# The mixture-of-experts stage of a two-block network on one core: expert by expert over all tokens, or token-expert pairs sorted into blocks of 128 slots

## The reference, cut to what matters

```python
grp_logits = t @ w_grp + b_grp                      # 4 groups
g_sel      = top_k(grp_logits, 1)
p_grp      = softmax(grp_logits)[g_sel]
in_grp     = (t @ w_exp + b_exp)[g_sel]             # 8 experts of the group chosen
top_val, top_idx = top_k(in_grp, 2)
top_w      = softmax(top_val) * p_grp
...
for gi in range(4):                                 # 8 experts each, 32 in all
    hid = silu(t @ w1[gi]) * (t @ w3[gi])           # 1024 -> 256 per expert
    out = out + (hid * gate[:, gi]) @ w2[gi]        # 256 -> 1024
h = h + g2 * out;  return rmsnorm_2(h, final_norm)
```

## Time and profile before

| | us |
|---|---|
| median of 3 runs | 3089.29 |
| lowest, highest | 3083.87, 3097.57 |
| span of the profiled execution | 3076.1 |
| median less span: launch and end, outside the records | 13.2 |
| stage of the experts, router to the end of the last `down` | 2503.8 to 3059.1 |
| tail, from there to the end of the span | 3059.1 to 3076.1 |

### The profile page before, as it was taken

One profiled execution on the slowest core, in us unless ns is written; L12 is line 12 of the kernel. 1 busy time (PEld: TensorE's weight loads), 2 busy tenths in 40 slices (PEclk: granted clock), 3 DMA queues, 4 the chain that ended last, 5 costly groups with the idle time before them and its releaser, 6 DMA issues.

```text
span 3076.1 us, 59430 instructions
## 1 busy us (share of the span) xinstructions
PE 2952.3 (96%) x19108; PEld 2680.6 (87%) x19108; DVE 2087.5 (68%) x3812; ACT 1582.8 (51%) x3113; POOL 1342.8 (44%) x1069
## 2 busy tenths in 40 slices
PE   7999999988999998999999799999999999999998
PEld 6689999986778877999999777878899889999997
DVE  7647963358888877589203888888654557777777
ACT  1125554468555555555555865555564335555554
POOL 5733888887544420069898855444000010000100
PEclk8999999999999998999999999999999999999999
DMA  6634556731666642445567037665354345555554
GB/s 247 214 105 152 183 195 249 271 131 55 253 232 230 227 139 70 139 151 184 180 209 259 27 141 267 234 226 203 131 183 136 120 137 192 191 193 192 202 191 144
DMA packets 153464, 552.60 MB, mean 180 GB/s; under 512 B 16896, under 2 KB 19712, under 8 KB 153232
## 3 DMA queue, kind: packets, MB, share of 16 engines
q1 hardware_dynamic: 151136, 547.42, 51.8%
q10 hardware_dynamic: 2224, 3.87, 0.4%
HBM read 550.17 MB, written 1.05 MB: 179 GB/s over the span
## 4 chain that ended last, share of the span: by engine, by line
PE 80%; ACT 8%; DVE 4%; POOL 3%; issue 3%; DMA 1%; ACTq 0%; DVEq 0%; POOLq 0%; SPq 0%
PE bank L1042 22%; PE bank L1012 21%; PE bank L1295 12%; PE bank L746 9%; PE bank L1316 5%; PE bank L805 5%; ACT hT L1528 3%; POOL w_parts L2656 2%; ACT hT L1524 1%; PE bank L770 1%; ACT h_parts L1536 1%; PE bank L691 1%; POOL arena L2704 1%; DMA ring<-stream 1%; PE bank L833 1%
## 5 line engine op out<-in xcount | busy, mean ns | idle before, releaser
L2656 POOL TENSOR_TENSOR w_parts<-ring,w_parts 128x512 fp32r<-128x512 f32 x512 | 660.6, 1308 | 407.6 <-ACT w_parts L1488 376.1
L1012 PE MATMUL bank<-h_parts,w_parts 128*128 128x256 f32 x6144 | 751.8, 284 | 6.0 <-ACT arena L1424 4.4
L1012 PEld LDWEIGHTS bank<-h_parts,w_parts 128*128 128x128 f32 x6144 | 743.3, 193 | 7.0 <-issue 4.8
L1488 ACT ACTIVATE w_parts<-ring 128x512 fp32r<-128x512 f32 x512 | 319.6, 631 | 344.5 <-PE bank L1012 273.7
L1710 ACT ACTIVATE w_parts<-ring 128x512 fp32r<-128x512 f32 x384 | 242.0, 632 | 262.6 <-PE bank L1295 129.9
L1295 PEld LDWEIGHTS bank<-h_parts,w_parts 128*128 128x128 f32 x3072 | 373.4, 192 | 2.6 <-issue 0.2
L1295 PE MATMUL bank<-h_parts,w_parts 128*128 128x256 f32 x3072 | 374.4, 283 | 0.0
L2586 DVE TENSOR_TENSOR w_parts<-ring,w_parts 128x512 fp32r<-128x512 f32 x376 | 273.1, 739 | 145.3 <-ACT w_parts L1710 142.0
L1042 PE MATMUL bank<-w_parts,a_parts 128*128 128x512 f32 x1536 | 370.6, 397 | 0.4 <-DVE a_parts L2291 0.4
L1042 PE MATMUL bank<-h_parts,a_parts 128*128 128x512 f32 x1536 | 365.3, 393 | 5.0 <-DVE a_parts L2291 5.0
L1042 PEld LDWEIGHTS bank<-h_parts,a_parts 128*128 128x128 f32 x1536 | 284.7, 188 | 78.2 <-DVE a_parts L2291 20.4
(11 more groups left out here) (347 smaller groups left out, 4455.5 us busy)
## 6 DMA issues: line engine op xcount, KB each, us to landing
ring<-stream SPq DMA_DIRECT2D x786, 512.0 KB, 3.4
arena<-stream SPq DMA_DIRECT2D x144, 512.0 KB, 4.3
hT<-stream SPq DMA_DIRECT2D x80, 512.0 KB, 4.6
mean<-stream SPq DMA_DIRECT2D x32, 512.0 KB, 4.5
arena<-consts ACTq DMA_DIRECT2D x1, 1536.0 KB, 6.4
xT<-xin ACTq DMA_DIRECT2D x1, 1024.0 KB, 10.7
out<-hT SPq DMA_DIRECT2D x4, 256.0 KB, 2.2
arena<-subk ACTq DMA_DIRECT2D x2, 128.0 KB, 2.1
```

The costliest lines, as they stand in the source:

```text
L1012: mm = pe.matmul(bank[k][:, 0:T], w[:, wp, ws], h_parts[:, hp, 4 * j + q, :], start=(j == 0 and q == 0 and i == 0), stop=(j == 1 and q == ...
L1488: act.activation(w_parts[half % HALVES][:, 0, :], ring[slot_][:, j * 512:(j + 1) * 512], ACT.Copy).then_inc(sem(f"{n}_high"), 1)
L2656: pool.tensor_tensor(w[:, 1, :], ring[(base + k) % RING][:, j * 512:(j + 1) * 512], w[:, 0, :].bitcast(F32), ALU.subtract).then_inc(sem(f" ...
```

## The change

The 512 pairs are given slots 0 to 511 in the order of their experts, and the slots are cut into four blocks of 128. An expert's pairs can lie on both sides of a boundary between blocks. There are three boundaries, so there are 32 + 3 = 35 steps, each of one expert and one block. Which expert and block a step has is computed on the chip; the number of steps is fixed.

- **Before the steps.** The tokens are transposed (16 transposes) and split. Five small products with a matrix of ones and a strictly triangular one (`below`) count the pairs ahead of each pair. VectorE makes one-hot matrices `E.first` and `E.sort` from these positions (256 tokens x 512 slots), and a table of integers `E.steps`. TensorE gathers the tokens into slot order with 32 fp32r matmuls of 512 columns; the result goes to `E.xs`, high part by ScalarE, low part by VectorE. There are 24 and 8 calls of `keep_clock` between.
- **A step.** Now the block's 128 slots stand in the array and the weights move through: 24 fp32r matmuls of 512 columns give all of x·w1 and x·w3. VectorE multiplies silu, the gate of the slot and the other half in one operation. Two transposes turn the hidden values, and w2 is multiplied in plain float32, 4 products of 512 columns. VectorE adds the result into the block's part of `E.y`. GpSimd copies the next block's tokens (`E.xb`, two copies of 128 x 1024).
- **Loads.** w1 and w3 of a step come in one transfer of 2 MB, w2 in one of 1 MB. Each has two buffers. Their rows in `stream` are read from `E.steps` into a register (`value_load`) by SP. VectorE and GpSimd read their block from it likewise.
- **After the steps.** `E.y` is split and multiplied with the transposed `E.sort`, 8 matmuls of 256 columns for each of 8 chunks, in the place of the two transposes a chunk.

The loops over steps below are SP's, TensorE's, ScalarE's, VectorE's and GpSimd's, in this order.

```diff
+BLOCKS = TT * 2
+STEPS = NE + BLOCKS - 1
+PARTED = 3
...
+            def up_load(p, row):
+
+                sp.dma_start(E.raw[:, p % 2].rearrange("p h s n -> p s (h n)"), stream[row].rearrange("s p n -> p s n"))\
+                  .then_inc(sem(f"v_landed{p % 2}"), 16)
...
+            for p in range(3, STEPS):
+                row = step_row(UP_ROW, p)
+                sp.wait_ge(sem("e_low"), 2 * p - 4)
+                up_load(p, bass.ds(row, 4))
+                row = step_row(DOWN_ROW, p - 1)
+                sp.wait_ge(sem("e_down"), 2 * (p - 2))
+                down_load(p - 1, bass.ds(row, 2))
+                if p in MOE_ROWS_AT:
+                    mod_load(MODS_MOE, MODS_MOE[0] + MOE_ROWS_AT[p])
...
+            keep_clock(pe, 24)
+            pe.matmul(t[:, 0:NE], ones, E.both[:, 0, :], start=True, stop=False)
...
+            keep_clock(pe, 8)
...
+                for q in range(4):
...
+                    for i, (x, wp) in enumerate(((0, 0), (0, 1), (1, 0))):
+                        mm = pe.matmul(o, step_x(p, x, 4 * h + q), E.hl[u % PARTED][:, wp, :, q * P:(q + 1) * P],
+                                       start=(h == 0 and q == 0 and i == 0), stop=(h == 1 and q == 3 and i == 2))
...
+            for p in range(STEPS):
+                if p + 1 < STEPS:
+                    up(p + 1, 0)
+                turned(p)
+                if p + 1 < STEPS:
+                    up(p + 1, 1)
...
+                down(p)
...
+            for p in range(STEPS):
+                silu(p)
+                if 2 * p + 4 < UNITS:
+                    high(2 * p + 4)
+                hidden_turned(p)
+                if 2 * p + 5 < UNITS:
+                    high(2 * p + 5)
...
+            for p in range(STEPS):
+                hidden(p)
+                if 2 * p + 4 < UNITS:
+                    low(2 * p + 4)
+                if p:
+                    add_up(p - 1)
+                if 2 * p + 5 < UNITS:
+                    low(2 * p + 5)
...
+            for p in range(1, STEPS):
+                at = pool.value_load(E.steps[0:1, SLOT_AT, p:p + 1], min_val=0, max_val=(BLOCKS - 1) * P)
+                if p >= 2:
+                    pool.wait_ge(sem("e_half"), 2 * (p - 1))
+                for x in range(2):
+                    ins = pool.tensor_copy(E.xb[:, p % 2, x, :, :], E.xs[x][:, :, bass.ds(at, P)])
```

More of the change, by code:

```diff
@@ L116 @@
            ("decay", RH * 384)]
+CONSTS_E = [("slots", 512), ("below", 128)]
 def offsets(table):
@@ L1341, in _ @@
+            for c in (DC - 2, DC - 1):
+                square_sum_pe(pe, "out", c)
         @block.tensor
@@ L1734, in moe_act @@
             act.wait_ge(sem("e_gexp"), signalled("e_gexp"))
-            highs(range(2, 3), same, same)
+            high(0)
             act.wait_ge(sem("e_vx"), 1)
```

562 lines of the change are left out of this document (346 added, 216 removed).

## The result

The kernel after takes 2908.40 us (median of 4 runs, 2906.18 to 2910.65) against 3086.58 for the kernel before in the same runs (3082.32 to 3097.57). The ratio is 0.9422, with a 95% interval of 0.9393 to 0.945: 5.8% faster. The forecast was 2934, with a range of 2903 to 3015. As a difference it was 155.7 us less; the medians differ by 178.2 and the two profiled spans by 169.2.

A forecast was written before the change was run, and what follows sets the result against it. TensorE was taken to bound the changed stage, with VectorE then setting 10.0 us a step. Lead-in, first step, 34 steps and tail made the span 155.7 us less; 3089.3 - 155.7 gave about 2934 us, range 2903 to 3015.

The forecast's parts named there:

- first step and gates: Start of the steps: two units of 2.82, 16 plain products (6.2) and 8 transposes (1.4), 13.2 us.
- 34 steps, last turn and `down`: Expert steps: 34 x 10.0 us, and 4.3 for the last turn and `down` with their wait.
- tail: After the last `down`: last addition and splits 2.1, eight chunks 11.5, 8.3 after the last square sum; 21.9 us.
- time less span: Whole kernel: the median lies 13.2 us above the profiled span, added at the end.
- VectorE's sum: Step on VectorE: 6.8 us, plus 2.0 for subtractions stretched by GpSimd's copies and 1.2 for register reads, 10.0 us.
- TensorE alone, 9.44: Rival for the steps: TensorE sets 9.44 us a step, 19 us less, 2915; chance 0.50 together with the forecast.
- TensorE's own step: Step on TensorE: 24 wide products 5.63, `down` 3.45, two transposes 0.36; 9.44 us against 16.98 an expert.
- The transfers: Steps, DMA: 8.7 to 9.5 us a step, close behind the limit; as rival setting the step 2971 us, chance 0.17.
- VectorE locked out: Rival for the steps: every GpSimd copy excludes every subtraction, 11.9 us a step, 65 more, 2999 us; chance 0.24.
- The slower rival: 2 MB loads: pieces 512 KB apart run below the ring's rate; 3288 us if nothing overlapped, chance 0.06.
- The lead-in: Between router and steps: first `up` at 2541.0 against 2512.2, 28.8 us lost.
- the signs named: Steps' profile: 9.9 to 10.1 us, TensorE near 95%, DMA share above 0.85; wrong if landings exceed 12 us.

The follow-up runs named there:

- experiment 1: Against the change: GpSimd's copies of the next block's tokens left out, with TensorE's wait for them; 2911.1 us, step 9.316 us.
- experiment 7: Against the change: VectorE's two register reads a step left out, gate and block taken by step number; 2912.6 us, step 9.416 us.
- experiment 4: Against the change: half of the `down` products and all matrix loads after the third step left out; 2853.7 us, step 7.886 us.
- experiment 2: Against the change: matrices loaded only for the first steps, modulation rows kept; 2904.9 us, step 9.180 us.
- Experiments 2 and 5: The second of these, against the change: two further plain products of 256 columns a step on TensorE, results unread; 2936.0 us, step 10.007 us.
- experiment 8: Against the change: the w2 load issued by ScalarE's queue instead of SP's; 2906.7 us, step 9.233 us.
- 10 to 12: The last of these, 12, is the kernel of experiment 11 run again, unchanged; 2900.1 us, step 9.249 us.
- experiment 6: Against the change: the 2 MB load as four transfers of 512 KB, each contiguous; 2915.9 us, step 9.367 us.
- experiment 3: Against the change: half of the `down` products left out, all loads kept; 2890.6 us, step 8.905 us.
- experiment 9: Against the change: before the steps, GpSimd's four subtractions wait until positions are known, 11 clock-keeping products instead of 24; 2911.8 us.
- experiment 11: Against the change: first two units split during the mixer, memset after the gates, 11 clock-keeping products, w2 load by ScalarE's queue; 2892.6 us.
- experiment 10: Against the change: the edits of experiment 8 and experiment 9 together; 2905.0 us, step 9.180 us.

## Why the prediction was right, point by point

The forecast was right: 2908.4 lies in the range, near its low end and 25.6 under the forecast. The reason held that TensorE had bound the stage and has 128 slots instead of 256 tokens to compute; that VectorE would take over as the limit did not. Term by term, in us:

| term | predicted | measured |
|---|---|---|
| router's start | 2503.80 | 2507.95 |
| from there to the first `up` | 37.2 | 39.1 |
| first step and gates | 13.2 | 10.0 |
| 34 steps, last turn and `down` | 344.3 | 325.3 |
| tail | 21.9 | 24.5 |
| time less span | 13.2 | 1.8 |

The rows add up: 4.15 + 1.9 - 3.2 - 19.0 + 2.6 = -13.5, which is 2906.9 less 2920.4; with 11.4 less around the span it is 24.9 between the forecast before rounding (2933.6) and the profiled execution's 2908.73.

- **The step that failed is VectorE's sum.** "The step I take: 10.0 us, set by VectorE" was wrong: it is 9.43 and TensorE sets it. Its 2.0 us for GpSimd's copies measured 4 x (1.54 - 1.18) = 1.4 for all of GpSimd's work, and some 1.0 for the copies by experiment 1; the 1.2 for register reads measured nothing (experiment 7). The subtraction alone was 1.18, not 1.23. With that VectorE has 6.14 + 1.28 + 0.47 = 7.9 us a step, from the groups above, and experiment 4 gives the same 7.9. The rival "TensorE alone, 9.44" named the right mechanism. That its number is so near 9.43 is luck: TensorE's own step is 9.18, and the 0.25 above it comes from late loads, which that rival does not have.
- **TensorE's own step** was 9.44 in the prediction and 9.18 in experiment 2, since by the chain the 24 wide products take 0.231 each and not 0.235, and the two transposes 0.21 together and not 0.36. `down` at 3.45 was right (3.43).
- **The transfers.** 8.7 to 9.5 was the estimate and 8.9 is measured. They were said to be close behind, and they are: they cost 0.25 us a step, by the loop through SP's queue that the prediction describes. It had given both loads 10.4 us from the first issue to the last landing and so had 2 us to spare in the loop; the 2 MB load alone took 9.8 in the median and up to 12.2, and at the place shown the last landing came 13.0 us behind the first issue (2708.77 to 2721.75). Experiments 2 and 5 show the cost from both sides, and experiment 8 with 10 to 12 that some 0.17 of it is the order in SP's queue.
- **VectorE locked out** (0.24) falls as the limit of the steps. GpSimd's copy, priced at 1.93 after an operation with two inputs, takes 1.04 alone (2547.74 in the trace of the kernel after) and 2.03 beside the subtractions. Both engines lose in the loop, and the copies' share costs the steps 0.1 us or less (experiment 1). One loss does reach the path, beside work that the prediction called hidden: GpSimd's modulation rows, which hold VectorE up so that TensorE waits 0.7 to 1.1 us in four of the steps, when the load before was late.
- **The slower rival,** pieces 512 KB apart at less than the ring's rate, falls by experiment 6 and by 366 GB/s in experiment 3. The Trainium skill (DMA: Bandwidth & Descriptors, the table of latency and other measured facts) gives 207 GB/s at that pitch; its case has the rows of neighbouring partitions that far apart, while here the pieces within a partition are, and neighbours lie 4 KB apart. The bound drawn from it does not hold for this source, by these runs.
- **The lead-in** came 1.9 us later than foreseen, relative to the router. TensorE reached the five counting products as priced (20.1 us behind the router, 20.3 foreseen), at 2528.05. Then VectorE took longer:

```profile
2520.63 3.56 DVE L2706 TENSOR_TENSOR arena<-arena 128x64 f32<-128x64 f32 x2
...
2521.73 9.30 POOL L2882 TENSOR_TENSOR e_parts<-arena,e_parts 128x1024 fp32r<-128x1024 f32 x4
...
2524.23 2.27 DVE L2710 TENSOR_TENSOR arena<-arena 128x64 f32<-128x64 f32 x1
...
2530.95 3.53 POOL L2884 MEMSET ring<- 128x4096 f32 x1
...
2531.60 3.55 DVE L2725 TENSOR_SCALAR e_first<-mean,rope_c 128x512 fp32r<-128x512 f32 x2
...
2547.06 0.70 PE L1413 MATMUL bank<-e_parts,w_parts 128*128 128x512 f32 x2 [1.05 <-ACT w_parts L1562]
```

The first two comparisons took 3.55 where 0.88 is their own time (experiment 9), until the memset ended at 2534.48. The 3.56 and 2.27 us for products of 64 elements ahead of them lie beside GpSimd's subtractions; with those elsewhere they take 1.36 and 0.22 (experiment 11). The Trainium skill (SBUF — State Buffer, the part on who interferes with whom) says that one of the two engines is blocked for the other's whole instruction, and names as affected operations with two SBUF inputs, copies and those with a scalar, but not a reduction. The traces agree: the reduction between the stalled operations takes 0.26 in experiment 9, as elsewhere. The prediction had applied the rule only to the steps, where it costs little, and not to the lead-in, where it costs 2 us.
- **The gates** were priced at 6.2 for 16 plain products; their 32 records took 3.49. The price came from the router's 32 records (6.25), which ran at a granted clock of 0.77 in the mean, and the gates at 1.00.
- **The tail** was 2.6 longer: 13.3 for the eight chunks instead of 11.5 and 0.8 more until the first of them (2885.25). The 8.3 behind the last square sum held (2898.57 to 2906.9).
- **Around the span.** The 13.2 us were not launch and end. The profiled executions of 2908.73 us (span 2906.9) and 3082.57 (span 3080.8, a run of the kernel before) have 1.8 around it. With 1.8 around it the profiled execution of before would have some 3077.9 us, an estimate, under the lowest time in its table (3083.87): it was one of the fastest, and the text ahead of the prediction took its distance from the median for something else.

Of the signs named, these showed: DMA share above 0.85, ScalarE's idle time released by a DMA, landings of 9.8 us in the median, subtractions of 1.18 and of 1.6 instead of 2.2. The longest landing was 12.2, just over the 12 named as a sign of being wrong. ScalarE's idle time was to say that the transfers set the step; it shows though TensorE does, so this sign does not part the two. TensorE is busy for 98% and not 95%.

## What to carry to other kernels

A stage whose chain is one engine alone gets shorter by what that engine has less to do. Before adding extras to another engine's sum of busy time, ask which of them overlap with its own work, and measure the order of the limits by taking work from two of them in turn, then from both. One wait in a queue delays every load behind it; with transfers at nine tenths of their share this was the first thing to show here. An engine that a late load has robbed of its lead is then open to a stall that costs nothing otherwise. Small operations of VectorE stall behind GpSimd as long as large ones: where they stand on the path, give GpSimd's work another time, and look at what it meets there, for here the first try only moved the stall.

## What the runs showed of the hardware that was not expected

- Operations of 3 and of 35 elements on VectorE took 2.00 and 5.70 us beside GpSimd's subtractions and a memset, which reads nothing; casts from a bank stayed at 0.69.
- A register read by SP took 0.27 us, and those of VectorE showed in no time at all.
- One core's transfers kept up 366 GB/s over 275 us.
- The start of the router moved by 17 us between executions, at code that nearly all of these kernels share. It is as large as the gain of experiment 11, which is why that gain shows in the stages and hardly in the medians. The longer executions have the lower mean granted clock.
- In experiment 10 the granted clock fell to 0.57 for 8 us while TensorE was busy, where the same work in experiment 9 had 1.00, and cost 2.8 us.
